# A decoder step in split float32: the high and low halves of the weights in two plain arrays instead of interleaved

## The reference

```
h = RMSNorm(x);  u, B, C, q/k/v of 3 head groups, g_a, g_b = split(h @ w_in)     2048 -> 11776
A = (B * causal_conv3(C * u)) @ w_conv_out                                       1024 -> 2048
Battn = merge(softmax attention of the 3 dilated groups) @ w_attn_out            512 -> 2048
x = x + (sigmoid(g_a) * A + sigmoid(g_b) * Battn) @ w_out                        2048 -> 2048
up, gate = split(RMSNorm(x) @ w_ffn_in)                                          2048 -> 11264
x = x + (silu(causal_conv3(gate) + b) * up) @ w_ffn_down;  y = RMSNorm(x)        5632 -> 2048
```

## Time and profile before

| | |
|---|---|
| median of three runs | 1504.68 us (1503.13 to 1504.70) |
| the profiled execution | 1503.96 us, its span 1502.3 us |
| TensorE, busy | 1491.9 us, 99% of the span |
| DVE, busy | 910.9 us, 61% |
| ACT, busy | 745.0 us, 50% |
| POOL, busy | 79.3 us, 5% |
| granted TensorE clock | 0.998 of 2.4 GHz |

### The profile page before, as it was taken

The page is one execution under the profiler, slowest core; times in us unless marked ns, Lnnn a source line. Parts: engine busy times, 40 slices in busy tenths (PEclk is TensorE's granted clock), DMA queues, the critical chain, the costliest instruction groups (busy, mean ns, idle before and its releaser), DMA issues.

```text
span 1502.3 us, 31560 instructions
## 1 busy us (share of the span) xinstructions
PE 1491.9 (99%) x12434; PEld 1489.8 (99%) x12434; DVE 910.9 (61%) x1157; ACT 745.0 (50%) x756; POOL 79.3 (5%) x145
## 2 busy tenths in 40 slices
PE   9999999999999999999999999999999999999998
PEld 9999999999999999999999999999999999999998
DVE  6748587756666446666666565664444656556454
ACT  7555554444555344455555454454444545445453
POOL 0300001001221000100000000000000000000000
PEclk9999999999999999999999999999999999999999
DMA  8677666556888766555587776775555666565553
GB/s 278 231 240 242 184 206 224 154 167 204 247 253 250 248 179 182 179 183 174 179 259 244 248 231 215 252 248 189 183 183 181 181 183 182 179 187 192 185 182 109
DMA packets 145913, 308.58 MB, mean 205 GB/s; under 512 B 10480, under 2 KB 11120, under 8 KB 145280
## 3 DMA queue, kind: packets, MB, share of 16 engines
q1 hardware_dynamic: 139296, 267.68, 56.6%
q0 software_dynamic: 5920, 38.05, 7.6%
q10 hardware_dynamic: 576, 1.05, 0.2%
HBM read 301.32 MB, written 26.38 MB: 218 GB/s over the span
## 4 chain that ended last, share of the span: by engine, by line
PE 98%; DVE 1%; DMA 0%; ACT 0%; SPq 0%; issue 0%; DVEq 0%
PE acc L1072 71%; PE acc L1084 8%; PE acc L1082 8%; PE acc L1083 8%; PE side L1172 0%; PE side L1193 0%; DMA x_in<-x_fm 0%; PE side L1240 0%; DVE yg L1047 0%; DVE w_split L642 0%; PE side L1183 0%; PE acc L1116 0%; PE acc L1098 0%; PE acc L1100 0%; PE acc L1122 0%; PE acc L1099 0%
## 5 line engine op out<-in xcount | busy, mean ns | idle before, releaser
L401 ACT ACTIVATE w_split<-raw 128x1024 fp32r<-128x1024 f32 x501 | 589.2, 1183 | 653.6 <-PE acc L1072 530.3
L642 DVE TENSOR_TENSOR w_split<-raw,w_split 128x1024 fp32r<-128x1024 f32 x501 | 614.0, 1233 | 481.0 <-ACT w_split L401 475.5
L1072 PE MATMUL acc<-h_rows,w_split 128*128 128x264 f32 x6432 | 786.0, 284 | 0.0
L1072 PEld LDWEIGHTS acc<-h_rows,w_split 128*128 128x128 f32 x6432 | 778.4, 194 | 0.2
L1072 PE MATMUL acc<-f_rows,w_split 128*128 128x264 f32 x1704 | 206.2, 284 | 0.0
L1072 PEld LDWEIGHTS acc<-f_rows,w_split 128*128 128x128 f32 x1704 | 205.5, 194 | 0.0
L1084 PE MATMUL acc<-h_rows,w_split 128*128 128x264 f32 x712 | 203.3, 285 | 0.0
L1083 PE MATMUL acc<-h_rows,w_split 128*128 128x264 f32 x712 | 202.5, 284 | 0.0
L1082 PE MATMUL acc<-h_rows,w_split 128*128 128x264 f32 x712 | 202.4, 284 | 0.0
L1084 PEld LDWEIGHTS acc<-h_rows,w_split 128*128 128x128 f32 x712 | 138.1, 194 | 0.0
L1083 PEld LDWEIGHTS acc<-h_rows,w_split 128*128 128x128 f32 x712 | 137.8, 193 | 0.0
(11 more groups left out here) (219 smaller groups left out, 1038.0 us busy)
## 6 DMA issues: line engine op xcount, KB each, us to landing
raw<-w_in SPq DMA_DIRECT2D x181, 512.0 KB, 3.9
raw<-w_ffn_in SPq DMA_DIRECT2D x176, 512.0 KB, 4.3
raw<-w_ffn_down SPq DMA_DIRECT2D x88, 512.0 KB, 3.7
raw<-w_out SPq DMA_DIRECT2D x32, 512.0 KB, 3.7
s_kv<-cache POOLq DMA_DIRECT2D x16, 1020.0 KB, 8.9
raw<-w_conv_out SPq DMA_DIRECT2D x16, 512.0 KB, 4.9
raw<-w_attn_out SPq DMA_DIRECT2D x8, 512.0 KB, 3.7
s_kv<-cache POOLq DMA_DIRECT2D x8, 508.0 KB, 4.8
```

The costliest lines, as they stand in the source:

```text
L401: act.activation(w_hi[:, s % RING], raw[:, s % RING], ACT.Copy).then_inc(hi_ready, 1)
L642: dve.tensor_tensor(w_lo[:, s % RING], raw[:, s % RING], w_hi[:, s % RING].bitcast(F32), ALU.subtract).then_inc(lo_ready, 1)
L1072: mm = pe.matmul(backwards(acc[:, m, 0:T]), w[:, slot, k, m * P:(m + 1) * P], row, start=False, stop=False)
```

## The change

The one array `w_split` goes; `w_hi` and `w_lo` become arrays of their own with the same shape as the views had. Together they take as many bytes as before, so nothing that is placed after them moves. ACT, DVE and the weight loads now touch neighbouring 4-byte elements; a weight load of 128 columns reads 512 bytes instead of 128 elements out of 1024. All instructions, waits and transfers stay the same.

```
         raw = place("raw", [P, RING, 2, GW])
-        w_split = place("w_split", [P, RING, 2, GW, 2], F32R)
-        w_hi, w_lo = w_split[:, :, :, :, 0], w_split[:, :, :, :, 1]
+        w_hi = place("w_hi", [P, RING, 2, GW], F32R)
+        w_lo = place("w_lo", [P, RING, 2, GW], F32R)
         h_at = cursor[0]
```

## The result

The kernel with two plain arrays takes 1522.9 us (median of 4 runs, 1522.7 to 1523.55). The kernel before, run beside it, takes 1504.6 us (1503.13 to 1504.7). The ratio is 1.0127, with a 95% interval of 1.0112 to 1.0142: 19 us slower. The profiled execution has a span of 1522.0 us against 1502.3.

What follows compares the result with a forecast made beforehand. TensorE's matmul pace was taken as the bound: 1503.96 - 0.5 (ACT at the start) + 20.3 (lost pace) = 1523.8 us profiled, about 0.7 more for the median, 1524.5; range 1416 to 1545 us.

Steps and rivals of the forecast that it cites:

- The bound: TensorE's matmuls, busy 1491.9 of 1502.3 us and 98% of the chain of waits, set the run's time.
- The cover: ACT and DVE changes hidden by idle time before lines 401 and 642 (653.6 and 481 us); transfers neither gain nor lose.
- The 0.5 us gain in the first 40 us: ACT's cheaper conversions at line 401 count only at the start, where ACT is busy 32.2 of 40 us: 0.5 us off.
- The load gets shorter, the pitch does not: Weight loads on `w_split`: each some 3 to 6 ns shorter, but the split matmul itself holds the array about 120 ns.
- rows 5 and 6: Trace around line 1193: plain load behind a split matmul still waits 0.12 to 0.13 us; interleaved loads there take 120 ns.
- The fast rival: The 8-byte-step load bounds the split matmuls; plain loads give a 113 ns pitch, 1422 us; chance 0.22.
- The lost pace: Split matmuls out of step with plain loads: 2.0 ns on 8904 at line 1072, 1.0 ns on 2500, 20.3 us; chance 0.41.
- The rest have the effect already: Split matmuls outside the 8904 and 2500 counted, such as on unplaced `att` and `t` rows, lose nothing more.
- the case that gave it: Slower by the lost pace: 1524 us, own range 1508 to 1546, chance 0.41.
- That effect on a middle chunk is not in the trace: Middle-chunk loss was only bounded, from a 7.3 ns gain to a 3.0 ns loss per matmul; 2.0 ns taken.
- No placing can keep the two in step: Plain load sweeps 512 bytes while the matmul beside it sweeps 1056, so no row placement avoids the lost pace.
- The rule against it: Trainium skill: TensorE's read ports are independent and it never waits, so plain arrays can't be slower: 1503.5 us or less.

Runs made afterwards that it cites:

- With 240 columns: Kernels before and after, middle chunks leaving out the first 24 of 264 columns (output incomplete), one execution each: interleaved 1485.4 us, plain 1444.4 us.
- the rows in two blocks: Changed kernel, `h_rows` and `f_rows` as all high halves, then all low halves, tiles 1152 bytes apart, starting at 0 or 128 modulo 256: 1503.15 us.
- PLACE = 128: Kernel before (interleaved weights), high halves of `h_rows` and `f_rows` starting at 128 modulo 256 bytes, not 224: 1522.35 us, ratio 1.0121.
- The two kernels with rows at 64 and at 32: Changed kernel with `h_rows` and `f_rows`: high half at 64, low at 96 modulo 256: 1518.1 us; low half first at 32, high at 64: 1513.2 us.
- PLACE = 64: Changed kernel (plain weights), high halves of `h_rows` and `f_rows` starting at 64 modulo 256 bytes, not 224: 1518.1 us, ratio 1.0092.

## Why the prediction was right, and where it was not

**The bound.** "Nothing else can shorten or lengthen the run by much unless it changes the pace of the matmuls": the page shows it, 19.2 of 19.7 us in TensorE's busy time.

**ACT and DVE.** ACT was forecast at about 1050 ns and stands at 1058; DVE at 1225 to 1235 and stands at 1232 (1258 ns scaled by 1024 / 1056 is 1220, not the prediction's 1225; nothing hangs on it). The cover held: ACT's idle time before these conversions rose from 653.6 to 730.8 us, so what it saved it spent waiting for TensorE. The 0.5 us gain in the first 40 us did not show; the first split matmul starts at 6.38 us instead of 5.81, which the profile after doesn't tie to the change and which is about the rest of the 19.7 us.

**The load gets shorter, the pitch does not.** Right, and the reading of rows 5 and 6 was right with it. Behind a split matmul at line 1193, the changed kernel shows 0.12 us again:

```profile
255.30 0.98 PEld L1193 LDWEIGHTS side<-prob_t,vtok 128*128 128x128 f32 x8
255.42 1.05 PE L1193 MATMUL side<-prob_t,vtok 128*128 128x128 f32 x8
...
256.20 0.19 PEld L1072 LDWEIGHTS acc<-h_rows,w_hi 128*128 128x128 f32 x1
256.20 0.30 PEld L1072 LDWEIGHTS acc<-h_rows,w_hi 128*128 128x128 f32 x2
```

Behind the last plain matmul of line 1193 the next two loads now start 0.11 us apart (one record lasts 0.19 us, both together 0.30), where the interleaved ones of the earlier trace rows stood 0.12 apart. With 240 columns the two sides came apart as that reading says: 118 ns for the interleaved load, 112 or less for the plain one, 120 for the matmul at 264. The fast rival fell on this: its condition, a split matmul with a pitch under 120 ns at 264 columns, holds as a mean in no kind of chunk in any run. The rule of the Trainium skill, "TensorE: Matmul & The Clock Gate", section "Back-to-back issue gap" (columns / 2.4 + 2.5 ns), would give 112.5 ns; the page offers it for a lone matmul and says that in a stream of loads and matmuls both have a part in the spacing. Here the lowest steady pitch in a stream is 120.0 ns, and with 240 columns and plain weights it is 112.2 ns where the formula gives 102.5, so the traces do not bear it out for float32r.

**The lost pace: +2.0 ns in middle chunks, +1.0 in first and last.** Measured +1.9 and +1.7 on `h_rows` and `f_rows`. The 20.3 us of the sum stand against 19.2. "The rest have the effect already" held roughly: the rest moved by +0.5 and +0.6 (`t` and `ab` rows, middle) and by -0.4 to -0.9 (`att`, `ab` and `t` rows, first and last), and the two chunk orders are a little nearer to each other, 0.6 ns apart instead of 0.8.

That the size came out is luck, and the case that gave it had a chance of 0.41 in the prediction. "That effect on a middle chunk is not in the trace" was a misreading: the trace before has 768 middle matmuls on unplaced rows (`t` and `ab`), at 120.3 and 120.1 ns, and the placed rows stand at 120.3. By the prediction's own rule, that the matmuls lose what the unplaced ones lose now, the middle chunks would have lost nothing. In the first and last chunks the unplaced rows stood 0.8 to 1.1 ns above the placed ones, not the 2.0 of the one chunk in the earlier trace rows. The profile after says the same from the other side: in its middle chunks the unplaced rows are the fast ones, at 120.7 and 120.8 against 122.2.

**The reason given for it was wrong.** "No placing can keep the two in step": the rows in two blocks bring plain weights to 1503.15 us. What the change took away is the match between this row placement and this step of the weights. Shown by four runs in a square: placement of before with interleaved weights 1504.6 and with plain ones 1522.9, two-block placement with plain weights 1503.15 and with interleaved ones 1519.7 (the kernel before took 1503.95 beside these two). How step and placement act on each other inside the chip no run shows.

**The rule against it.** The Trainium skill, "SBUF — State Buffer", section "Who interferes with whom", has the two read ports of TensorE independent and TensorE never waiting. The runs speak against it at the scale of a few ns: the place of the rows and the direction of reading alone move the same instructions between 1503 and 1535 us. The 16-byte lines of the same page of the Trainium skill, of which it wants at least two hits each for full bandwidth, fit the largest step: from 8 to 16 bytes, where each line holds one wanted element instead of two, the load's pitch, ACT and DVE all go up steeply (118 to 233 ns, 1183 to 2094, 1233 to 2082). But two hits are not quite free either: from 4 to 8 bytes ACT pays 125 ns.

**Open.** Why a given pair of addresses runs flat or alternates. With interleaved weights a start at 128 was slow in three layouts (`t` rows, PLACE = 128, two blocks); for plain weights no such rule held on all rows. The two kernels with rows at 64 and at 32 show that what came before a chunk has a part in it; no run here isolates it.

## What to carry to other kernels

When two streams feed TensorE, weights and moving rows, a change of the layout of one asks for a new placement of the other; judge a layout only after moving the rows' start by a few multiples of 32 bytes, since here up to 19 us came and went by that alone. Moving them once and seeing little (PLACE = 64) doesn't show that no place is good. Before paying for a cheaper load, find which side holds the pitch, by shortening the matmul by some columns for a timing (the output is then incomplete): here the plain load is worth nothing at 264 columns and 41 us at 240. Don't let the step of float32 operands grow from 8 to 16 bytes: that alone took this kernel to 2867 us.

## What the runs showed of the hardware

- A step of 16 bytes instead of 8 takes the weight load from a pitch of about 118 to 233 ns, a 128x1024 conversion that ACT writes from 1183 to 2094 ns, and the subtraction of DVE, which reads one operand and writes with that step, from 1233 to 2082 ns. From 4 to 8 bytes ACT pays 125 ns (1058 to 1183) and DVE nothing.
- A float32r matmul of 264 columns has a lowest steady pitch of 120.0 ns, 10 ns over its columns at 2.4 GHz, with weights of 4 and of 8 bytes step. With 240 columns and plain weights it is 112.2 ns, 12 over; whether the matmul or the load holds it there, the runs don't tell.
- Plain-weight matmuls on rows at the same place modulo 256 bytes ran in more than one steady pattern, flat at 120 or alternating 120 and 126 to 127 ns, within one execution.
- With interleaved weights, rows that start at 128 modulo 256 bytes run at some 123 ns, rows at 0 at 120 to 121.
- Reading the moving rows backwards instead of forwards (and writing the accumulator backwards with them) is worth 12 to 24 us here.
